# Comparison numbers in PSUM, attention heads in pairs, queries scaled at their eviction: a three-block fp32 kernel on one Trainium2 core

## The chip, the cores and the metric

The kernel runs on one core of one Trainium2 chip. Its time is the device time of one execution in microseconds (us). The core's engines each work through an instruction list of their own and meet only at semaphores: PE (TensorE, matrix products), DVE (VectorE), ACT (ScalarE), POOL (GpSimd) and SP (SyncE, which here issues DMAs). Two on-chip memories matter: SBUF, and PSUM with its eight banks, into which PE writes and from which DVE and ACT read.

## The reference

A first block of two layers, then a second block of one layer. 256 tokens x and 256 context tokens ctx, width 1024, everything in fp32.

```python
# first block, each layer: ffn, mixer, ffn on x (and on ctx in layer 0); the mixer's attention part:
s_loc = einsum(q, k_block) * scale + bias           # scale = 64 ** -0.5 = 0.125, 8 heads of 64
s_ctx = einsum(q, k_ctx) * scale
p = softmax(concat([s_loc, s_ctx]), axis=-1)        # o = p_loc @ v + p_ctx @ v_ctx
# in layer 0 the context too attends to itself:
p = softmax(einsum(q, k) * scale); o = p @ v
# second block: retention, a sparse attention, then the expert retrieval:
s = einsum('btphd,phnd->btphn', q, subkeys)         # 8 heads, 2 halves, 128 keys
v, i = top_k(s, 16)
cand = v[..., 0, :, None] + v[..., 1, None, :]      # 256 pairs a head
cidx = i[..., 0, :, None] * 128 + i[..., 1, None, :]
tv, tj = top_k(cand, 16)
eidx = take_along_axis(cidx, tj); w = softmax(tv)   # 8 * 16 = 128 experts a token
a = gelu(einsum(h, w_down[eidx]));  out = einsum(w * a, w_up[eidx])
```

## The kernel before, in words

**Weights.** All weights stream in as units of 128x1024 (512 KB) by DMA. For fp32 accuracy each is split: ACT rounds it to a high part (L174), DVE (L181) or, in one stretch, POOL (L231) subtracts for the low part, and a product is three matmuls (L262, L263, L264). Such a unit is a *down*, *up* or *query* unit below; one of 24 matmuls is worked on in two halves of 12.

**Order.** Nothing schedules at run time. Each class has a method for each engine, whose text is the instruction order; semaphores hold the engines together. Where side work lies between weight units is set by constants in the text.

**Mixer attention** (`Mix`, L1200 on, once a layer). `MixIn.scalar` (L1182) evicts the projections, queries included, from PSUM. The scores are worked as *items*: one head and 128 queries each; 16 local items (256 local and 256 context keys: 512 columns) in each layer and, in layer 0 alone, 16 context items (256 columns). For an item w: PE makes the scores in bank w % 2 (L1276: a head has 64 channels, so the matmul uses 64 of the array's 128 rows); DVE multiplies by 0.125, adds the bias on the local half (L1376), multiplies the other half (L1377; L1380 for a context item), and takes the maximum (L1383); ACT takes the exponential (L1328, and its sum is read out); DVE normalises (L1391, L1392); PE transposes 128x128 pieces (L1286) into bank 2 or 3; ACT copies them out (L1338); PE multiplies them by the values (L1298, 64 output channels of a head, for two items at once, into bank 4 or 5); ACT moves the result (L1346). The items' order is head by head. Semaphore waits let PE be at most three score items ahead.

**Retrieval** (`Retrieve`, L1955 on). PE runs 16 query units, then K0 = 47 of the 128 down units. Beside the down units the other engines find the experts. DVE takes the top 16 of each head's keys, makes the 256 candidate sums of each head (`pairs`, L2205 and L2208), takes their top 16 (`choose`), and turns the positions into key numbers by comparing with a row of numbers 0 to 127, the iota (`decode`, L2223 to L2238: L2227 is the comparison, L2232 a product, L2234 a sum). `weights` (L2244 to L2246) ends the softmax. All of it is done for two halves of 128 tokens, tt = 0 and 1. Then PE turns the slots (`turn`, L2030), and a dense table of 128 x 128 weights a token is built in 64 *batches* of 4 tokens: DVE *compares* the iota with both key numbers of a slot (L2170, 128x1024 to SBUF), POOL *weighs* one of the two one-hot matrices (L2137, 128x512), PE *spreads* (L2039: 4 matmuls, their outer products, in one of banks 4 to 7) and ACT *keeps* the result (L2082). Compare may run six batches ahead of the spread, by the buffers.

**Constants.** From down unit ALONE = 22 on there is one batch per half unit, for 16 units; then PAUSE = 2 units without any; then two batches per half until K0, which is 7 units; the last 4 batches follow alone. In this whole stretch POOL both weighs and subtracts (L231), until the last units, whose subtraction DVE does. `turn(0)` stands at the end of unit ALONE-1. The second half's `choose` and `decode` run on DVE between comparisons of the first half's batches (`more`). After that `Experts` works through the other 81 down units and 128 up units. Down results of `Retrieve` go to DRAM and come back later (47 of each).

Of the kernel before, what the change touches and what calls it, by code (L numbers as in the profile page):

```python
# [21 lines left out]
ALU = mybir.AluOpType  # L22
# [3 lines left out]
P = 128  # L26
# [372 lines left out]
A_POOL = A_PT + 2048  # L399
# [717 lines left out]
class MixIn:  # L1117
# [60 lines left out]
    def scalar(self, act):  # L1178
# [23 lines left out]
class Mix:  # L1202
    def __init__(self, chip, layer, last, mix_in):
# [3 lines left out]
        self.sc, self.pt = chip.part(A_SC, 4, 512), chip.part(A_PT, 2, 4, S)  # L1207
# [7 lines left out]
        self.items = [(g, h, qt) for g in range(ng) for h in range(NA_H) for qt in range(2)]  # L1215
        n = len(self.items)
        self.scored, self.scores_read, self.maxed, self.exped, self.probs, self.turned, self.copied = (
            s.take(n) for s in (chip.scored, chip.scores_read, chip.maxed, chip.exped, chip.probs, chip.turned, chip.copied))
        self.product, self.moved, self.mixed = chip.product.take(n // 2 + 1), chip.moved.take(n // 2), chip.mixed.take(1)
        self.y_there = chip.y_there.take(2)  # L1220

    def keys(self, g):
        return (0, T2) if g == 0 else (S, T2)

# [40 lines left out]
    def tensor(self, pe):  # L1265
# [4 lines left out]
        def scores(w):  # L1270
            g, h, qt = items[w]
            lo, hi = keys(g)
            po, q0 = 64 * (h % 2), g * S + qt * P
            if w >= 2:
                pe.wait_ge(self.scores_read.sem, self.scores_read.at(w - 1))
            nc.tensor.matmul(chip.bank[w % 2][:, 0:hi - lo], u[po:po + 64, CH_Q + h // 2, q0:q0 + P],  # L1276
                             u[po:po + 64, CH_K + h // 2, lo:hi], start=True, stop=True)\
                .then_inc(self.scored.sem, 1)
# [11 lines left out]
        def values(n):  # L1290
            g, h, _ = items[2 * n]
            po = 64 * (h % 2)
            pe.wait_ge(self.copied.sem, self.copied.at(2 * n + 2))
            if n >= 2:
                pe.wait_ge(self.moved.sem, self.moved.at(n - 1))
            nkt = (keys(g)[1] - keys(g)[0]) // P
            for kt in range(nkt):
                mm = nc.tensor.matmul(chip.bank[4 + n % 2][po:po + 64, 0:S],  # L1298
# [1343 lines left out]
```

## Time and profile before

| | |
|---|---|
| median of 3 runs | 3045.37 us (3043.37 to 3047.05) |
| profiled execution | 3047.02 us, its span 3045.2 us |
| mean granted PE clock | 0.975 of full speed |
| busy share of the span | PE 94%, DVE 71%, ACT 40%, POOL 18% |
| mixer of layer 0, first score to last values | 562.9 to 642.6 us |
| mixer of layer 1, the same | 1549.4 to 1601.5 us |
| retrieval, first spread to the first matmul of `Experts` | 2221.4 to 2415.4 us |

All times of places are from the start of the span. An engine's busy time is the sum over its instructions; where an instruction waited, the timeline gives the idle time before it and, behind an arrow, the engine and line that released it. A tile name (extension_mixer, arena, bank) covers many buffers: arena is the reused part of SBUF, bank is PSUM. A matmul in fp32 as L1276's and L1298's stands as two records in the timeline, and records that follow each other without a gap may be drawn together, with a count.

### The profile page before, as it was taken

The numbers are of one execution on the slowest core, as the hardware profiler recorded it, in microseconds if no ns is written. First come the engines' busy times: TensorE is split into PE (matmuls) and PEld (weight loads), VectorE is DVE, ScalarE is ACT, GpSimd is POOL, SyncE is SP. The second block draws the span as 40 slices with busy tenths as digits, with TensorE's granted clock in tenths as the row PEclk, the third lists the DMA queues.
The fourth block names the chain that finished last, engine by engine and source line by source line (L and its number), as shares of the span: only waits on it lengthen the run. The fifth ranks groups of instructions, "written<-read, shape, count | busy, mean of one in ns | idle before, by whom it ended". The sixth has DMA issues, their size and how long they took to land. (4 is left out here: it accounts for less than half of the span.)

```text
span 3045.2 us, 40386 instructions
## 1 busy us (share of the span) xinstructions
PE 2862.2 (94%) x15682; PEld 2391.7 (79%) x15682; DVE 2171.0 (71%) x3813; ACT 1225.8 (40%) x2228; POOL 534.0 (18%) x403
## 2 busy tenths in 40 slices
PE   7999999999999999999899999389977899999997
PEld 4888878568888778888859999259967788888886
DVE  2999994558998975657656665446997777777776
ACT  2322243453222342223445455245544444444444
POOL 1111115000111110001400000003899600000000
PEclk9999999999999999999999999689999999999999
DMA  6445542123545454444414555304633356555553
GB/s 237 179 174 193 187 151 90 49 92 137 180 176 197 152 191 163 156 147 160 144 42 140 185 188 168 114 1 140 189 107 100 97 189 192 193 190 189 195 190 118
DMA packets 121295, 463.05 MB, mean 152 GB/s; under 512 B 13456, under 2 KB 26128, under 8 KB 107792
## 3 DMA queue, kind: packets, MB, share of 16 engines
q1 hardware_dynamic: 107280, 359.79, 35.9%
q0 software_dynamic: 13824, 100.67, 8.5%
q8 instruction: 125, 2.05, 0.3%
q14 instruction: 66, 0.54, 0.1%
HBM read 453.20 MB, written 7.21 MB: 151 GB/s over the span
## 5 line engine op out<-in xcount | busy, mean ns | idle before, releaser
L174 ACT ACTIVATE weight_hi<-weight_ring 128x512 fp32r<-128x512 f32 x1272 | 798.6, 631 | 1197.5 <-PE bank L264 1196.0
L181 DVE TENSOR_TENSOR weight_lo<-weight_ring,weight_hi 128x512 fp32r<-128x512 f32 x1154 | 868.7, 756 | 466.8 <-ACT weight_hi L174 465.1
L262 PE MATMUL bank<-operand_hi,weight_hi 128*128 128x256 f32 (+1 forms) x3168 | 1046.7, 330 | 28.5 <-DVE operand_lo L601 13.0
L263 PE MATMUL bank<-operand_lo,weight_hi 128*128 128x256 f32 (+1 forms) x3168 | 1036.8, 327 | 0.0
L264 PE MATMUL bank<-operand_hi,weight_lo 128*128 128x256 f32 (+1 forms) x3168 | 1036.1, 327 | 0.0
L262 PEld LDWEIGHTS bank<-operand_hi,weight_hi 128*128 128x128 f32 x3168 | 606.2, 191 | 95.7 <-issue 21.4
L263 PEld LDWEIGHTS bank<-operand_lo,weight_hi 128*128 128x128 f32 x3168 | 606.3, 191 | 52.7
L264 PEld LDWEIGHTS bank<-operand_hi,weight_lo 128*128 128x128 f32 x3168 | 606.0, 191 | 50.4
L859 DVE SCALAR_TENSOR_TENSOR extension_ffn<-extension_ffn,silu_c 128x512 f32<-128x512 f32 x532 | 388.0, 776 | 1.7
L262 PE MATMUL bank<-hidden_hi_ffn,weight_hi 128*128 128x512 f32 (+1 forms) x704 | 256.6, 364 | 4.0 <-DVE arena L1104 4.0
L263 PE MATMUL bank<-hidden_lo_ffn,weight_hi 128*128 128x512 f32 (+1 forms) x704 | 255.3, 363 | 0.0
L264 PE MATMUL bank<-hidden_hi_ffn,weight_lo 128*128 128x512 f32 (+1 forms) x704 | 255.3, 363 | 0.0
L262 PE MATMUL bank<-weight_hi,act_hi_experts 128*128 128x512 f32 x512 | 214.3, 419 | 0.0
L263 PE MATMUL bank<-weight_lo,act_hi_experts 128*128 128x512 f32 x512 | 200.7, 392 | 0.0
L264 PE MATMUL bank<-weight_hi,act_lo_experts 128*128 128x512 f32 x512 | 200.1, 391 | 0.0
L231 POOL TENSOR_TENSOR weight_lo<-weight_ring,weight_hi 128x512 fp32r<-128x512 f32 x118 | 188.9, 1613 | 50.5 <-ACT weight_hi L174 49.4
L810 POOL DMA_DIRECT2D extension_ffn<-in_w_mods x88 | 53.6, 612 | 715.9 <-DVE extension_ffn L859 589.6
L826 POOL TENSOR_TENSOR mod_lo_ffn<-extension_ffn,mod_hi_ffn 128x1024 fp32r<-128x1024 f32 (+1 forms) x44 | 98.3, 2233 | 428.0 <-ACT mod_hi_ffn L868 428.0
L262 PEld LDWEIGHTS bank<-hidden_hi_ffn,weight_hi 128*128 128x128 f32 x704 | 132.8, 189 | 28.5 <-DVE arena L1104 6.7
L264 PEld LDWEIGHTS bank<-hidden_hi_ffn,weight_lo 128*128 128x128 f32 x704 | 132.8, 189 | 20.8
L263 PEld LDWEIGHTS bank<-hidden_lo_ffn,weight_hi 128*128 128x128 f32 x704 | 132.9, 189 | 20.5
L2170 DVE TENSOR_TENSOR arena<-iota,arena 128x1024 f32<-128x1024 f32 x64 | 121.9, 1927 | 17.2 <-PE bank L2039 16.5
(259 smaller groups left out, 2807.6 us busy)
## 6 DMA issues: line engine op xcount, KB each, us to landing
weight_ring<-in_ffn SPq DMA_DIRECT2D x272, 512.0 KB, 3.5
weight_ring<-in_experts SPq DMA_DIRECT2D x256, 512.0 KB, 3.5
extension_ffn<-in_w_mods POOLq DMA_DIRECT2D x96, 1024.0 KB, 7.6
weight_ring<-in_w_mix SPq DMA_DIRECT2D x56, 512.0 KB, 3.4
weight_ring<-in_w_second SPq DMA_DIRECT2D x52, 512.0 KB, 4.0
spill<-early_retrieve SPq DMA_DIRECT2D x47, 128.0 KB, 3.8
arena<-spill SPq DMA_DIRECT2D x47, 128.0 KB, 3.5
extension_mixer<-in_rel_bias SPq DMA_DIRECT2D x2, 1536.0 KB, 6.7
```

Source lines behind the costliest of these rows:

```text
L174: nc.scalar.activation(self.hi[:, g % 2, h], self.ring[:, g % NS, h], ACT.Copy).then_inc(self.rounded, 1)
L181: self.nc.vector.tensor_tensor(self.lo[:, g % 2, h], self.ring[:, g % NS, h], self.hi[:, g % 2, h].bitcast(F32), ALU.subtract).then_inc(se ...
L231: self.nc.gpsimd.tensor_tensor(self.lo[:, g % 2, h], self.ring[:, g % NS, h], self.hi[:, g % 2, h].bitcast(F32), ALU.subtract).then_inc(se ...
L262: nc.tensor.matmul(out, a_hi, b_hi, start=start and n == 0, stop=False)
L263: nc.tensor.matmul(out, a_hi, b_lo, start=False, stop=False)
L264: last = nc.tensor.matmul(out, a_lo, b_hi, start=False, stop=stop and n == len(pairs) - 1)
L810: pool.dma_start(self.w[:, j, u, :, :], src).then_inc(self.loaded[j].sem, 16)
L826: nc.gpsimd.tensor_tensor(self.lo[:, 0:n], self.flat(j), self.hi[:, 0:n].bitcast(F32), ALU.subtract)\
L859: ins = nc.vector.scalar_tensor_tensor(acc, w, scale, acc, ALU.mult, ALU.add)
L2170: nc.vector.tensor_tensor(self.hots(b), iota[:, :].unsqueeze(1).unsqueeze(1).to_broadcast([P, BATCH, 2, P]), self.columns[:, 0:2, t:t + BA ...
```

## The change

- **Queries.** They are multiplied by 0.125 as ACT evicts them. DVE's two instructions on a local item's scores become an addition of the bias and a copy. A context item needs none any more: the maximum and the exponential read the scores in their bank. PE's next context scores wait for the exponential now, not for DVE's copy.
- **Paired heads.** Items are ordered by pairs of heads, the two heads of a pair next to each other. Their score matmuls, on array rows 0 to 63 and 64 to 127, are issued back to back into two banks out of 0, 1, 6, 7. The value matmuls of four items (two heads, 256 queries) are issued in four parts, one behind each item's transposes, the two heads alternately on columns 0 to 63 and 64 to 127 of bank 4 or 5. There is one move per four items, on 128 partitions. The transposed probabilities have twice the buffers.
- **Numbers in PSUM.** ACT copies the iota once into bank 7; `compare` and `decode` read it there. The spreads have banks 4 to 6 instead of 4 to 7.
- **Constants and order.** K0 is 45 instead of 47, ALONE 20 instead of 22. `pairs(1)` is split: heads 0 to 3 before `weights(0)`, heads 4 to 7 behind it.

PE in the attention of layer 0, steady state, local items (L1276 becomes L1289 in the changed kernel, the scores; L1286 becomes L1299, transposes; L1298 becomes L1315, values). Two items before:

```order
L1276 MATMUL bank<-extension_mixer 128x512
L1286 MATMUL bank<-ident,extension_mixer 128x128 x4
L1276 MATMUL bank<-extension_mixer 128x512
L1286 MATMUL bank<-ident,extension_mixer 128x128 x4
L1298 MATMUL bank<-extension_mixer 64x256 x4
```

and two items now:

```order
L1289 MATMUL bank<-extension_mixer 128x512 x2
L1299 MATMUL bank<-ident,extension_mixer 128x128 x4
L1315 MATMUL bank<-extension_mixer 64x256 x2
L1299 MATMUL bank<-ident,extension_mixer 128x128 x4
L1315 MATMUL bank<-extension_mixer 64x256 x2
```

The number of matmuls is the same; the two score matmuls stand together, and the four of values stand as two pairs, each behind one item's transposes.

DVE before the first comparison of the retrieval (L2205 and L2208 are `pairs`, L2244 to L2246 `weights(0)`, on which PE's `turn(0)` waits). Before:

```order
L2238 TENSOR_TENSOR arena<-arena 128x128
L2205 CAST arena<-arena 128x256
L2208 TENSOR_TENSOR arena<-arena 128x256 x8
L2244 TENSOR_REDUCE arena<-arena 128x8
L2245 RECIPROCAL arena<-arena 128x8
L2246 TENSOR_TENSOR arena<-arena 128x128
L2189 MAX arena<-arena 128x8 x2
L2170 TENSOR_TENSOR arena<-iota,arena 128x1024
```

and now:

```order
L2266 TENSOR_TENSOR arena<-arena 128x128
L2233 CAST arena<-arena 128x256
L2236 TENSOR_TENSOR arena<-arena 128x256 x4
L2272 TENSOR_REDUCE arena<-arena 128x8
L2273 RECIPROCAL arena<-arena 128x8
L2274 TENSOR_TENSOR arena<-arena 128x128
L2236 TENSOR_TENSOR arena<-arena 128x256 x4
L2216 MAX arena<-arena 128x8 x2
L2197 TENSOR_TENSOR arena<-bank,arena 128x1024
```

Four of the candidate sums have gone behind `weights(0)`, and the comparison reads bank instead of iota. The diff, cut to its core:

```diff
-A_POOL = A_PT + 2048
+A_POOL = A_PT + 4096
-            nc.scalar.activation(self.u[:, n, 0:self.width[n]], chip.bank[n % 4][:, 0:self.width[n]], ACT.Copy)\
+            nc.scalar.activation(self.u[:, n, 0:self.width[n]], chip.bank[n % 4][:, 0:self.width[n]], ACT.Copy,
+                                 scale=DH ** -0.5 if CH_Q <= n < CH_K else 1.0)\
                 .then_inc(self.evicted.sem, 1)
...
-        self.items = [(g, h, qt) for g in range(ng) for h in range(NA_H) for qt in range(2)]
+        self.items = [(g, 2 * hp + j, qt) for g in range(ng) for hp in range(NA_H // 2) for qt in range(2) for j in range(2)]
+    def score_bank(self, w):
+        return (0, 1, 6, 7)[w % 4]
...
+        def scores(n):
+            if n >= 2 and 2 * n - 3 < self.local:
+                pe.wait_ge(self.scores_read.sem, self.scores_read.at(2 * n - 2))
+            elif n >= 2:
+                pe.wait_ge(self.exped.sem, self.exped.at(2 * n - 2))
+            for w in (2 * n, 2 * n + 1):
+                g, h, qt = items[w]
+                lo, hi = keys(g)
+                po, q0 = 64 * (h % 2), g * S + qt * P
+                nc.tensor.matmul(chip.bank[self.score_bank(w)][:, 0:hi - lo], u[po:po + 64, CH_Q + h // 2, q0:q0 + P],
+                                 u[po:po + 64, CH_K + h // 2, lo:hi], start=True, stop=True)\
+                    .then_inc(self.scored.sem, 1)
...
+        def values(n, part):
...
+            if part == 0:
+                pe.wait_ge(self.copied.sem, self.copied.at(4 * n + 4))
+                if n >= 2:
+                    pe.wait_ge(self.moved.sem, self.moved.at(n - 1))
+            for j in range(2):
+                h = items[4 * n + j][1]
+                mm = nc.tensor.matmul(chip.bank[4 + n % 2][64 * j:64 * j + 64, 0:S],
+                                      v[:, part + 4 - nkt, h * DH:(h + 1) * DH], self.turned_probs(n, j, part),
+                                      start=(part == 0), stop=(part == nkt - 1))
...
-                nc.vector.scalar_tensor_tensor(s[:, 0:S], bank[:, 0:S], 0.125, bias[:, h, r0:r0 + S], ALU.mult, ALU.add)
-                nc.vector.tensor_scalar(s[:, S:T2], bank[:, S:T2], 0.125, None, ALU.mult)\
-                    .then_inc(self.scores_read.sem, 1)
-            else:
-                nc.vector.tensor_scalar(s[:, 0:n], bank[:, 0:n], 0.125, None, ALU.mult)\
-                    .then_inc(self.scores_read.sem, 1)
-            dve.wait_ge(self.scores_read.sem, self.scores_read.at(w + 1))
-            nc.vector.tensor_reduce(chip.nmax[:, w % 4:w % 4 + 1], s[:, 0:n], AX.X, ALU.max, negate=True)\
+                nc.vector.tensor_tensor(s[:, 0:S], bank[:, 0:S], bias[:, h, r0:r0 + S], ALU.add)
+                nc.vector.tensor_copy(s[:, S:T2], bank[:, S:T2]).then_inc(self.scores_read.sem, 1)
+                dve.wait_ge(self.scores_read.sem, self.scores_read.at(w + 1))
+            nc.vector.tensor_reduce(chip.nmax[:, w % 4:w % 4 + 1], s if g == 0 else bank[:, 0:n], AX.X, ALU.max, negate=True)\
                 .then_inc(self.maxed.sem, 1)
...
-NQ, K0 = 16, 47
-ALONE, PAUSE = 22, 2
+NQ, K0 = 16, 45
+ALONE, PAUSE = 20, 2
...
+        self.iota = chip.bank[7][:, 0:P]
...
-            if b >= 4:
-                pe.wait_ge(self.kept.sem, self.kept.at(b - 3))
+            if b >= 3:
+                pe.wait_ge(self.kept.sem, self.kept.at(b - 2))
...
+            if n == 6:
+                act.wait_ge(self.table.sem, self.table.at(17))
+                nc.scalar.activation(self.iota, chip.iota[:, :], ACT.Copy).then_inc(self.table.sem, 1)
...
-            nc.vector.tensor_tensor(self.hots(b), iota[:, :].unsqueeze(1).unsqueeze(1).to_broadcast([P, BATCH, 2, P]),
+            nc.vector.tensor_tensor(self.hots(b), iota.unsqueeze(1).unsqueeze(1).to_broadcast([P, BATCH, 2, P]),
...
-        pairs(1)
+        pairs(1, 0, PH // 2)
         weights(0)
+        pairs(1, PH // 2, PH)
         choose(1, 0)
```

## Rows read from the trace of the kernel before

**Rows 1.** Windows: stretch, length, busy time (instructions) by engine, clock, DMA.
```profile
560.00:645.00 85.00, 77.08 (x273) 36.26 (x272) 52.14 (x146) 46.73 (x120) 0.00 (x0) 0.92 0.04 13
2220.00:2343.00 123.00, 92.41 (x696) 87.94 (x694) 106.95 (x114) 50.25 (x91) 121.51 (x70) 0.94 0.32 94
...
2414.00:3020.00 606.00, 605.27 (x3475) 522.83 (x3474) 435.98 (x798) 284.52 (x496) 0.00 (x0) 1.00 0.58 187
```

**Rows 2.** PE timeline, local attention: start, us, engine, line, op, [idle, releaser].
```profile
585.71 1.12 PE L1276 MATMUL bank<-extension_mixer 64*128 64x512 f32 x2
...
589.00 0.66 PE L1286 MATMUL bank<-ident,extension_mixer 128*128 128x128 f32 x4 [0.52 <-DVE extension_mixer L1392]
589.58 1.94 PE L1298 MATMUL bank<-extension_mixer 128*64 128x256 f32 x8
```

**Rows 3.** Timeline of DVE, the same stretch.
```profile
586.87 0.43 DVE L1376 SCALAR_TENSOR_TENSOR extension_mixer<-bank,extension_mixer 128x256 f32<-128x256 f32 x1 [1.70 <-PE bank L1276]
...
588.86 0.42 DVE L1376 SCALAR_TENSOR_TENSOR extension_mixer<-bank,extension_mixer 128x256 f32<-128x256 f32 x1
```

**Rows 4.** Timeline of PE, context attention, layer 0.
```profile
619.88 0.44 PE L1286 MATMUL bank<-ident,extension_mixer 128*128 128x128 f32 x2 [0.44 <-DVE extension_mixer L1392]
...
623.38 0.44 PE L1286 MATMUL bank<-ident,extension_mixer 128*128 128x128 f32 x2 [0.43 <-DVE extension_mixer L1392]
```

**Rows 5.** One line's instructions: count, ns min/median/max, first and last start, forms.
```profile
L1376 DVE SCALAR_TENSOR_TENSOR extension_mixer<-bank,extension_mixer x32: 413/418/426, 564.2 to 1592.4; 128x256 f32<-128x256 f32 x32
...
L1328 ACT ACTIVATE extension_mixer<-extension_mixer,nmax x48: 499/721/724, 566.9 to 1593.9; 128x512 f32<-128x512 f32 x32, 128x256 f32<-128x256 f32 x16
L1328 ACT ACTIVATION_READ_ACCUMULATOR extension_mixer<-extension_mixer,nmax x48: 185/187/193, 567.5 to 1594.5; 128x1 f32 x48
...
L1338 ACT ACTIVATE extension_mixer<-bank x48: 383/597/598, 570.3 to 1598.9; 128x512 f32<-128x512 f32 x32, 128x256 f32<-128x256 f32 x16
...
L1777 PE MATMUL bank<-arena x32: 370/370/390, 1999.4 to 2002.7; 64*128 64x15 f32 x32
```

**Rows 6.** The same view, for lines of the retrieval.
```profile
L2170 DVE TENSOR_TENSOR arena<-iota,arena x64: 1211/2054/2311, 2219.0 to 2409.3; 128x1024 f32<-128x1024 f32 x64
...
L2137 POOL TENSOR_TENSOR arena<-arena x64: 1028/2015/2032, 2220.3 to 2411.4; 128x512 f32<-128x512 f32 x64
...
L231 POOL TENSOR_TENSOR weight_lo<-weight_ring,weight_hi x118: 1262/1297/3325, 2096.4 to 2375.1; 128x512 fp32r<-128x512 f32 x118
...
L2208 DVE TENSOR_TENSOR arena<-arena x16: 411/1507/1520, 2156.8 to 2216.6; 128x256 f32<-128x256 f32 x16
```

**Rows 7.** Timeline of PE, expert retrieval, first spread to end.
```profile
2217.91 0.55 PE L2030 MATMUL bank<-ident,arena 128*128 128x128 f32 x3 [4.01 <-DVE arena L2246]
...
2221.42 2.08 PE L2039 MATMUL bank<-arena 128*128 128x128 f32 x8 [0.54 <-POOL arena L2137]
...
2314.64 1.06 PE L2039 MATMUL bank<-arena 128*128 128x128 f32 x8
...
2316.97 1.06 PE L2039 MATMUL bank<-arena 128*128 128x128 f32 x8
...
2333.75 0.36 PE L262 MATMUL bank<-operand_hi,weight_hi 128*128 128x256 f32 x1
...
2343.05 2.13 PE L2039 MATMUL bank<-arena 128*128 128x128 f32 x16 [1.82 <-POOL arena L2137]
...
2382.84 2.15 PE L2039 MATMUL bank<-arena 128*128 128x128 f32 x16
...
2386.26 2.15 PE L2039 MATMUL bank<-arena 128*128 128x128 f32 x16
...
2415.38 0.55 PE L262 MATMUL bank<-operand_hi,weight_hi 128*128 128x256 f32 x1 [0.73 <-issue]
```

**Rows 8.** Timeline of DVE: second half's decoding, its start and end.
```profile
2258.78 1.31 DVE L2223 TENSOR_SCALAR arena<-arena 128x128 uint32<-128x128 uint32 x1
...
2298.49 4.29 DVE L2170 TENSOR_TENSOR arena<-iota,arena 128x1024 f32<-128x1024 f32 x2
```

More of the change, by code:

```diff
@@ L1288, in transposes @@
             mm.then_inc(self.turned.sem, 1)
[L1290 to L1295, printed above, removed]
-            nkt = (keys(g)[1] - keys(g)[0]) // P
-            for kt in range(nkt):
-                mm = nc.tensor.matmul(chip.bank[4 + n % 2][po:po + 64, 0:S],
-                                      v[:, kt + 4 - nkt, h * DH:(h + 1) * DH], pt[:, n % 2, kt, :],
-                                      start=(kt == 0), stop=(kt == nkt - 1))
-            mm.then_inc(self.product.sem, 1)
+        def values(n, part):
+            g, _, _ = items[4 * n]
+            nkt = (keys(g)[1] - keys(g)[0]) // P
+            if part >= nkt:
+                return
+            if part == 0:
[7 more added lines that the diff above has]
+                                      start=(part == 0), stop=(part == nkt - 1))
+            if part == nkt - 1:
+                mm.then_inc(self.product.sem, 1)
         pe.wait_ge(evicted.sem, evicted.at(16))
-        for w in range(3):
-            scores(w)
+        scores(0)
         pe.wait_ge(evicted.sem, evicted.at(20))
+        scores(1)
         for w in range(len(items)):
-            if w + 3 < len(items):
-                scores(w + 3)
+            ahead = w // 2 + 2
+            early = 2 * ahead - 3 < self.local
+            if w % 2 == 0 and ahead < len(items) // 2 and early:
+                scores(ahead)
             transposes(w)
-            if w >= 2 and w % 2 == 0:
-                values(w // 2 - 1)
-        values(len(items) // 2 - 1)
+            if w % 2 == 0 and ahead < len(items) // 2 and not early:
+                scores(ahead)
+            if w >= 4:
+                values(w // 4 - 1, w % 4)
+        for part in range(4):
+            values(len(items) // 4 - 1, part)
         pe.wait_ge(self.mixed.sem, self.mixed.at(1))
@@ L1354, in scalar @@
             copies(w)
-            if w >= 3 and w % 2 == 1:
-                move(w // 2 - 1)
-        move(len(items) // 2 - 1)
-        act.wait_ge(self.product.sem, self.product.at(len(items) // 2 + 1))
+            if w >= 8 and w % 4 == 1:
+                move(w // 4 - 2)
+        move(len(items) // 4 - 2)
+        move(len(items) // 4 - 1)
+        act.wait_ge(self.product.sem, self.product.at(len(items) // 4 + 1))
         for b in range(2):
@@ L2082, in keep @@
             nc.scalar.activation(self.weight[:, BATCH * b:BATCH * (b + 1), :].rearrange("p a b -> p (a b)"),
-                                 chip.bank[4 + b % 4][:, :], ACT.Copy).then_inc(self.kept.sem, 1)
+                                 chip.bank[4 + b % 3][:, :], ACT.Copy).then_inc(self.kept.sem, 1)
         def exp(tt):
@@ L2201, in best, with pairs @@
                 dve.wait_ge(chip.dve_step.sem, chip.dve_step.base)
-        def pairs(tt):
-            step(nc.vector.tensor_copy(ixf[:, tt, :, :], ix[:, tt, :, :]))
+        def pairs(tt, first, last_h):
+            if first == 0:
+                step(nc.vector.tensor_copy(ixf[:, tt, :, :], ix[:, tt, :, :]))
             vp = v[:, tt, :, :].rearrange("p (h two) k -> p h two k", two=2)
-            for h in range(PH):
+            for h in range(first, last_h):
                 last = nc.vector.tensor_tensor(
```

52 lines of the change are left out of this document (25 added, 27 removed).

## The prediction

> **What bounds the kernel now.** I read the windows first [rows 1]. In the Experts stage PE is busy for 605.27 of 606 us: what stands there costs its full time. In the mixer of layer 0 it is busy 77.08 of 85 us, at a granted clock of 0.92, with DVE at 52.14: neither is full. From 2220 to 2343, in the retrieval, PE is busy 92.41 of 123 us and POOL 121.51: there POOL sets the pace. Then the timelines. In the mixer's local part PE waits 0.52 us for DVE's normalisation before a transpose [rows 2] and DVE waits 1.70 us for scores once in two items [rows 3]: each waits for the other in turn. Two items take 5.68 us: 2 x 1.99 (the distance from one item's first DVE instruction to the next) + 1.70 [rows 3]. In the context part two items take 3.50 us [rows 4]. In the retrieval the durations of one instruction stand far apart [rows 6]: the comparison L2170 takes 1.21 us at least and 2.05 in the median, the weighing L2137 1.03 or 2.02, the subtraction L231 1.26 to 3.33. A DVE instruction with two inputs in SBUF and a POOL instruction lengthen each other. When DVE rested (2311 to 2320), a half unit with its spread took 2.33 us, 2314.64 to 2316.97 [rows 7].
>
> **The mixers.** Bias addition and copy replace two DVE instructions of the same shape, L1376 at 0.42 us being the row for both sorts: I take their saving as nothing. What can change is the 1.70 us. PE's work for two items is two score matmuls (1.12 each, drawn as two records), two sets of transposes (0.66 each) and the values (1.94) [rows 2]: 5.5 as drawn, 5.2 without its 0.52 of waiting, since drawn times overlap a little (5.68 - 0.52). If both kinds of pairs ran side by side it would be 1.12 + 1.32 + 0.97 = 3.4, and with scores alone 4.4; DVE needs 3.98. So with both side by side DVE is the bound and the 1.70 goes; with scores alone most of it does. For side by side speaks L1777, on alternating halves of the rows: 32 matmuls of 0.37 us each within 3.6 us [rows 5], a third of their sum; but pipelined matmuls are drawn overlapped anyhow, and its halves of columns no row shows. Local items: 5.68 - 3.98 = 1.70 a pair, 8 pairs a layer: 13.6 at best. In layer 1 I take 12; in layer 0 only 9, since a clock of 0.92 [rows 1] and the first items' filling hold PE back there. Context items: four take 7.0 us now [rows 4]. ACT will be their bound, an exponential of 0.50 with 0.19 of reading its sum and a copy of 0.38 [rows 5], with a quarter of a move of about the copy's length 1.16 an item, 4.6 for four. 4 x (7.0 - 4.6) = 9.6, and 1 at the passage from local to context, whose items now go without a DVE copy: 10.5. The exponential may cost more or less from a bank; the copy L1338 reads one already and costs less than the exponential, so I take no difference. Sum of the mixers: -31.5. Bounds: -36 with both layers at the full 13.6 plus 9.6, and -11 if nothing runs side by side and only the reordering (0.5 a pair over 16 pairs) and part of the context's copy count.
>
> The Trainium skill, "TensorEngine Tiling (Array Packing)", Key Properties, says that tiles work in parallel, but that changing the tiling mode drains TensorE. Here the mode changes around each pair. By the first half of the rule the sum stands; by the second each change costs something that no row here isolates, and the time moves to the first rival's.
>
> **The comparison from PSUM.** 64 comparisons of 128x1024. The price of one from a bank is in no row. From below, 1.21 (the shortest from SBUF, no POOL beside it); from above 2.05, if nothing is freed. DVE reads a bank and SBUF in L1376, 256 elements in 0.413 us at least [rows 5]; L2208, two SBUF inputs of the same shape, takes 0.411 at least [rows 6]. So a bank costs nothing more by itself, and I take 1.22. The Trainium skill, "Perfetto Trace Analysis", Optimizing Scalar/DVE Operations, gives DVE some 125 ns of access overhead on PSUM against 60 on SBUF; by it the comparison would be 1.28 and 64 of them 4 us more, though hidden where PE sets the pace; the rows show 0.002 of difference, and I go by them.
>
> Does it free POOL? L2208 takes 0.41 at least and 1.51 in the median [rows 6], two SBUF inputs beside POOL's work; the same holds for L2170. L1376-like instructions stand beside no POOL work, so that a bank operand is free of it is inferred, not seen. The Trainium skill, "GPSIMD Engine Reference", Specifications, says that GpSimd's SBUF interface is shared with VectorE, with contention when a DVE instruction has two SBUF inputs or runs in a two-port mode. The comparison would then be out of it; the trace agrees as far as it goes (1.21 against 2.05).
>
> **The retrieval, step by step.** *Start* (places here are in the span of before, the mixers' gain apart). turn(0) waited 4.01 us for weights(0) [rows 7]; with two units less before it PE will wait there for 6 us more, or less by what DVE gains. DVE gains 0.8 us or more on each of the two decoding comparisons L2227. Four of the eight L2208 go behind weights(0), so that turn(0) comes sooner, but still ahead of the first comparison: they only fill the time of the turn and its eviction, about 0.5. And where PE waits, POOL runs out of subtractions, and the L2208 fall from 1.51 towards 0.41 [rows 6]: up to 4 us more. I put spread(0) at 2216.7 instead of 2221.42 [rows 7], between 2215.5 and 2218.7. *The 32 single batches.* Now 2221.42 to 2333.75, 112.3 us [rows 7]. PE's 2.33 a half is the floor, POOL's uncontended 1.04 + 1.27 = 2.31 just under it: 32 x 2.33 = 74.6. The decoding of the second half holds DVE from 2258.78 to 2298.49, 39.7 us, with 8 comparisons in it [rows 8]. With 8 x 0.83 less (2.05 to 1.22) and as much for each of two L2227, which have twice the elements (a cautious count), it is 31.4, or 3.9 a half, slower than PE by 12.8 over 8 halves; six batches of lead can hide that in part. 74.6 at best, 87.4 at worst; I take 82, nearer to the worst, since choose(1) keeps DVE from building much lead. *Pause*: 5 half units of 12 matmuls between spreads, 2333.75 to 2343.05, of which 1.82 was waiting for POOL [rows 7] and goes: 7.5, or 1.5 a half unit. *14 halves with two batches.* The stretch shows 3.42 a half once POOL has no subtraction left, 2382.84 to 2386.26 [rows 7]. POOL will need 2 x 1.04 + 1.27 = 3.35, DVE 2.5: 14 x 3.42 = 47.9. *The last 4*, from the last half to the first matmul of Experts: DVE alternates comparison 1.22 and subtraction 0.68, 1.9 each; 7.6 in all. So Experts begin at 2216.7 + 82 + 7.5 + 47.9 + 7.6 = 2361.7 instead of 2415.38 [rows 7]: -53.7. Three spread banks instead of four ask only that a batch be kept within three, and ACT needs 0.6 of each 2.33: nothing. The copy of the iota, one ACT instruction under query units: nothing. *Given back.* Two down units less stand before Experts and two more in it, where PE is full: 4 half units of 1.5 = 6.0. Retrieval: -47.7, bounds -57 (lead hides all, spread(0) early) and +2 (nothing is freed).
>
> **Sum.** 3047.02 - 31.5 - 47.7 = 2967.8 for the profiled execution, which stands 1.65 above the median of the runs shown; so 2966 as a median.
>
> **The rivals.** *A, the pairs don't run side by side.* For it: no row shows halves of columns in parallel, nor scores of 512 columns; PE then needs about 5.2 for two items and stays the bound. Mixers -11: 2986 to 2987. *B, POOL isn't freed* or the comparison is as long beside it. Against it is the sharp split of 1.04 and 2.02. The retrieval keeps its pace; the earlier start (-4) and the 6.0 given back leave +2: 3047 - 31.5 + 2 - 1.65 = 3016. *C, slower: the comparison from a bank is long.* Its broadcast read, the same numbers again for each slot, is no contiguous read as L1376's. The whole table then hangs on DVE: from spread(0) to Experts 64 x t plus some 62 us (the 194 of now, less 64 x 1.93, a mean between the median and the shorter ones [rows 6], is 70, of which 8 is waiting that falls away), against 194 now. Minus 31.5 and 5 of the start and plus 6, break-even is at t = (194 + 30.6 - 62) / 64 = 2.54; at 3.2, half as long again as the median now, the time is 3047 + 73 + 6 - 31.5 - 5 = 3089. Against it: 0.413 in [rows 5] and nothing near 2.5. *A and B together*: 3036.
>
> **Chances.** Forecast 0.60 (own range 2950 to 2980), A 0.18, B 0.12, A and B 0.04, C 0.03, and 0.03 for faster than 2950. The range of 8 in 10 is 2948 to 3002: it takes in A and the slower part of the forecast's costs and leaves out B's side. A difference under 0.2% (6 us) can't be told from none; faster 0.95, same 0.02, slower 0.03.
>
> **What would show it.** Local items 4.0 us apart per two, with DVE's 1.70 gone (A: 5 us, score records one behind another); context items at about 2.3 per two with ACT nearly full. The comparison (L2197 of the changed kernel) at 1.2 us in the median, the weighing always 1.04 (B: both still near 2); no waits of PE for POOL from unit ALONE on; Experts starting 85 us earlier in the span than before (31.5 + 53.7), and taking 6.0 us longer. The prediction is wrong if PE waits for more than 12 us at turn(0), if DVE's decoding holds back all 32 halves, or if the granted clock in these stretches falls to the lower level for long because PE now waits differently.

## The result, and the profile after

| | before | changed |
|---|---|---|
| median of runs | 3044.51 us (3043.37 to 3047.05, 4 runs) | 2948.94 us (2947.35 to 2950.94, 4 runs) |
| ratio | | 0.9685, 95% interval 0.9673 to 0.9697 |
| profiled execution | 3047.02 us | 2947.35 us |
| busy in the span: PE, DVE, ACT, POOL | 2862.2, 2171.0, 1225.8, 534.0 us | 2798.8, 2109.9, 1219.2, 464.5 us |

96 us faster; 2966 was forecast, 79 less than before. 2948.94 lies below the forecast's own range (2950 to 2980), in the part that it gave 0.03 to, and inside the range of 8 in 10 (2948 to 3002) by 1 us. The two profiled executions lie 99.7 us apart, one at the slow end of its runs, the other at the fast end. Where those 99.7 went, by the distance between equal places of the two spans, against the forecast's terms:

| stretch | forecast | traces |
|---|---|---|
| mixer of layer 0 | -19.5 | -25.1 |
| mixer of layer 1 | -12.0 | -14.5 |
| between it and the query units | 0 | -0.3 |
| start: to the first spread | -4.7 | -8.5 |
| 32 single batches and the pause | -32.1 | -32.9 |
| double batches and the last 4 | -16.8 | -22.1 |
| Experts | +6.0 | +3.7 |
| sum | -79.2 | -99.7 |

**Windows of the changed kernel**, columns as in [rows 1]: the mixer of layer 0, the single batches, Experts.

```profile
560.00:645.00 85.00, 72.44 (x367) 41.81 (x366) 58.18 (x153) 54.25 (x133) 2.24 (x4) 0.96 0.21 81
2173.00:2256.00 83.00, 78.19 (x648) 77.29 (x649) 76.42 (x106) 46.23 (x84) 76.33 (x64) 0.98 0.42 128
2312.00:2918.00 606.00, 606.00 (x3510) 524.85 (x3511) 437.34 (x799) 286.99 (x501) 0.00 (x0) 1.00 0.58 188
```

In the retrieval POOL is down from 121.51 of 123 us to 76.33 of 83 and PE up to 78.19 of 83: PE sets the pace. Experts is full of PE's work, as it was.

**PE in the local items**, the timeline that answers to [rows 2]:

```profile
584.34 1.13 PE L1289 MATMUL bank<-extension_mixer 64*128 64x512 f32 x4
585.40 0.66 PE L1299 MATMUL bank<-ident,extension_mixer 128*128 128x128 f32 x4
585.98 0.65 PE L1315 MATMUL bank<-extension_mixer 128*64 128x256 f32 x4
587.12 0.66 PE L1299 MATMUL bank<-ident,extension_mixer 128*128 128x128 f32 x4 [0.48 <-DVE extension_mixer L1415]
```

Two matmuls of scores, four records, take 1.13 us, where one, two records, took 1.12. Four records of values take 0.65 where eight took 1.94. PE waits 0.48 us for DVE's product, once in two items. DVE [rows 3] no longer waits for scores: from one item to the next it takes 1.98 us, without a gap.

```profile
585.00 0.42 DVE L1403 TENSOR_TENSOR extension_mixer<-bank,extension_mixer 128x256 f32<-128x256 f32 x1
...
586.98 0.42 DVE L1403 TENSOR_TENSOR extension_mixer<-bank,extension_mixer 128x256 f32<-128x256 f32 x1
```

**Context items** [rows 4]: two items that have value matmuls beside them take 2.53 us (602.06 to 604.59, 609.17 to 611.70), two without take 2.04 (607.13 to 609.17), in which PE waits 0.60 for DVE's product. Before, two took 3.50.

```profile
602.06 0.70 PE L1289 MATMUL bank<-extension_mixer 64*128 64x256 f32 x4
...
604.59 0.70 PE L1289 MATMUL bank<-extension_mixer 64*128 64x256 f32 x4
...
607.13 0.70 PE L1289 MATMUL bank<-extension_mixer 64*128 64x256 f32 x4
...
608.80 0.44 PE L1299 MATMUL bank<-ident,extension_mixer 128*128 128x128 f32 x2 [0.60 <-DVE extension_mixer L1415]
609.17 0.70 PE L1289 MATMUL bank<-extension_mixer 64*128 64x256 f32 x4
...
611.70 0.70 PE L1289 MATMUL bank<-extension_mixer 64*128 64x256 f32 x4
```

The value matmuls run four items late, so the first four context items still carry those of the last local ones. In that stretch PE has no gap:

```profile
596.00:608.00 12.00, 12.00 (x80) 5.53 (x76) 7.42 (x28) 9.11 (x33) 0.00 (x0) 1.00 0.00 0
```

**The comparison and the weighing** of the changed kernel, the view of [rows 6]: the two medians are 1.21 and 1.04, where they were 2.05 and 2.02.

```profile
L2197 DVE TENSOR_TENSOR arena<-bank,arena x64: 1198/1212/1226, 2170.6 to 2307.6; 128x1024 f32<-128x1024 f32 x64
...
L2164 POOL TENSOR_TENSOR arena<-arena x64: 1028/1041/3016, 2171.9 to 2308.9; 128x512 f32<-128x512 f32 x64
```

**The retrieval on PE**, answering to [rows 7]: turn(0), the first spread, two spreads where the second half's decoding begins, the first matmul of the pause, doubles, the last batches, the first matmul of Experts.

```profile
2168.60 0.90 PE L2054 MATMUL bank<-ident,arena 128*128 128x128 f32 x3 [4.56 <-DVE arena L2274]
...
2172.97 1.16 PE L2063 MATMUL bank<-arena 128*128 128x128 f32 x8 [0.91 <-POOL arena L2164]
...
2201.37 1.06 PE L2063 MATMUL bank<-arena 128*128 128x128 f32 x8
...
2203.70 1.06 PE L2063 MATMUL bank<-arena 128*128 128x128 f32 x8
...
2253.90 0.36 PE L262 MATMUL bank<-operand_hi,weight_hi 128*128 128x256 f32 x1
...
2261.70 2.13 PE L2063 MATMUL bank<-arena 128*128 128x128 f32 x16 [0.37 <-POOL arena L2164]
...
2265.10 1.95 PE L2063 MATMUL bank<-arena 128*128 128x128 f32 x16
...
2268.32 1.96 PE L2063 MATMUL bank<-arena 128*128 128x128 f32 x16
...
2303.77 3.74 PE L2063 MATMUL bank<-arena 128*128 128x128 f32 x32
2308.69 1.13 PE L2063 MATMUL bank<-arena 128*128 128x128 f32 x8 [1.19 <-POOL arena L2164]
...
2311.91 0.35 PE L262 MATMUL bank<-operand_hi,weight_hi 128*128 128x256 f32 x1 [0.73 <-issue]
```

The steps are 2.33 us (2201.37 to 2203.70) in the single batches and 3.22 (2265.10 to 2268.32) in the double ones. Experts begin at 2311.91 instead of 2415.38.

### The profile page after: what moved, and what is told of

It reads as the page before. It is cut to its first block and busy times, and to the rows that moved or that the text cites. A ratio compares the mean times of both kernels' runs of the same rounds, so it can differ in the third digit from the quotient of the medians.

```text
span 2945.5 us, 40330 instructions
## 1 busy us (share of the span) xinstructions
PE 2798.8 (95%) x15682; PEld 2359.6 (80%) x15682; DVE 2109.9 (72%) x3801; ACT 1219.2 (41%) x2217; POOL 464.5 (16%) x399
## 3 DMA queue, kind: packets, MB, share of 16 engines
q8 instruction: 125, 2.05, 0.3%
## 5 line engine op out<-in xcount | busy, mean ns | idle before, releaser
L231 POOL TENSOR_TENSOR weight_lo<-weight_ring,weight_hi 128x512 fp32r<-128x512 f32 x114 | 150.6, 1330 | 54.1 <-ACT weight_hi L174 52.7
L263 PEld LDWEIGHTS bank<-hidden_lo_ffn,weight_hi 128*128 128x128 f32 x704 | 132.9, 189 | 20.5
L262 PEld LDWEIGHTS bank<-weight_hi,act_hi_experts 128*128 128x128 f32 x512 | 95.9, 187 | 37.7 <-DVE act_lo_experts L272 12.0
```

The source lines that it names most:

```text
L231: self.nc.gpsimd.tensor_tensor(self.lo[:, g % 2, h], self.ring[:, g % NS, h], self.hi[:, g % 2, h].bitcast(F32), ALU.subtract).then_inc(se ...
L262: nc.tensor.matmul(out, a_hi, b_hi, start=start and n == 0, stop=False)
L263: nc.tensor.matmul(out, a_hi, b_lo, start=False, stop=False)
```

## The experiments

The runs of one group ran on one chip beside the kernel before; what a kernel is worth against the changed one is taken from the ratios to the kernel before.

### The parts alone

**The iota back in SBUF** (three spread banks, constants and order as changed):

```diff
-        iota16, iota = self.iota[:, 0:TOPK], self.iota
+        iota16, iota = chip.iota[:, 0:TOPK], chip.iota[:, :]
```

> The changed kernel with one thing undone: comparison and decoding read the iota in SBUF again (three spread banks, constants and order stay). Theory (the bank operand frees POOL and DVE of each other): the retrieval goes back to its old pace, comparison near 2.05 us and weighing near 2.0 in the median; the mixers keep their 40 us; about 3044.5 - 40 + 2 = 3006 us, between 3000 and 3012. Rival (the order, the split of pairs and the constants brought the retrieval's gain): 2950 to 2962 us.

Measured: 3005.37 us (ratio 0.9863, 0.9847 to 0.988). The page for the two lines, in the same view as above, shows the medians of before again:

```profile
L2197 DVE TENSOR_TENSOR arena<-iota,arena x64: 1206/2055/2314, 2176.2 to 2366.4; 128x1024 f32<-128x1024 f32 x64
...
L2164 POOL TENSOR_TENSOR arena<-arena x64: 1032/2016/2028, 2177.5 to 2368.6; 128x512 f32<-128x512 f32 x64
```

So this one operand carries 1.8% (0.9863 against 0.9685), some 54 us: that DVE and POOL hold each other up less is most of the retrieval's gain (59.8 in the table, from the start to Experts).

**The iota in a bank, and nothing else,** in the kernel before: ACT's copy, `self.iota` at the three places, banks `4 + b % 3`, `kept.at(b - 2)`; K0 = 47, ALONE = 22, `pairs(1)` whole, the mixers as before.

> The kernel before with the iota in a bank alone (three spread banks; K0 = 47, ALONE = 22, pairs(1) whole, mixers as before). Theory: the single batches 33 us shorter, the double ones and the last four 22, the start 4 to 6, the low clock at the start of Experts 2: about 2983 us, 2979 to 2987. Rival: constants and split carry a part of the gain of more than 10 us: above 2993 us.

Measured: 2984.69 us (ratio 0.9799, 0.9783 to 0.9815), 61.4 below the 3046.11 of before. Its DVE timeline at the start shows the decoding comparison at 2.29 us, but the eight candidate sums at 8.12, as long as before:

```profile
2186.21 2.29 DVE L2231 TENSOR_TENSOR arena<-bank,arena 128x2048 f32<-128x2048 f32 x1
...
2204.73 8.12 DVE L2212 TENSOR_TENSOR arena<-arena 128x256 f32<-128x256 f32 x8
```

**The mixers alone**: the file of the changed kernel up to the line `NQ, K0 = 16, ...`, from there on that of before.

> The mixers of the changed kernel with the retrieval of before. Theory: the spans of the two traces add up, 25.1 us from layer 0 and 14.5 from layer 1: 3044.5 - 40 = 3004.5 us, 3002 to 3007. Rival (the retrieval takes part of it back, as a transfer or the clock falls differently): above 3010 us.

Measured: 3008.16 us (ratio 0.9875, 0.9859 to 0.9892), 38.0 below before. The two parts add up to 99.4 on this chip, and the whole change measured 95.6 and 96.6 in its two comparisons. And the kernel with the iota in SBUF, which differs from this one by K0, ALONE, the split of pairs and the three banks, lies 2.8 below it. Neither of these differences, of opposite sign, is larger than the intervals: the constants and the order brought nothing that can be measured.

### The pairs of heads

**Neither rows nor columns in pairs**: the items' order within a pair of heads is head, query half, and each head's values are issued in turn.

```diff
-        self.items = [... for hp in range(NA_H // 2) for qt in range(2) for j in range(2)]
+        self.items = [... for hp in range(NA_H // 2) for j in range(2) for qt in range(2)]
...
-            for j in range(2):
-                h = items[4 * n + j][1]
+            for m in (2 * part, 2 * part + 1):
+                j, kt = m // nkt, m % nkt
+                h = items[4 * n + 2 * j][1]
...
-            at = S * (w % 2) + P * qt
+            at = S * (h % 2) + P * qt
```

> The changed kernel with items in the order head, query half within a pair of heads, so that back-to-back score matmuls use the same 64 rows, and with each head's value matmuls issued in turn, so that neighbours use the same columns. Banks, buffers, scaling, the move and all counts stay. Theory (the mixers' gain is matmuls running side by side): PE needs about 5.1 us for two local items and sets the pace; local items lose 1.1 us a pair over 16 pairs and context items about 1 a pair over 8: 26 us, about 2975 us, between 2968 and 2982. Rival (the deeper banks and the absent DVE copies brought it): at most 8 us lost, under 2957 us.

Measured: 2974.97 us (ratio 0.9766, 0.975 to 0.9783), 25 above the changed kernel. So of the mixers' 39.6 us, 25 are the pairs'; the other 15 go with what this run keeps (two banks of scores more, values in four parts, queries scaled at their eviction, no DVE copy for context items), and no run parts these from each other. The PE timeline of its local items: the same records, but the two scores take 1.98 us and a part of values 1.08, one behind another; two items are 5.1 apart (586.50 to 591.60).

```profile
586.50 1.98 PE L1289 MATMUL bank<-extension_mixer 64*128 64x512 f32 x4
...
589.00 1.08 PE L1316 MATMUL bank<-extension_mixer 128*64 128x256 f32 x4
...
591.60 1.12 PE L1289 MATMUL bank<-extension_mixer 64*128 64x512 f32 x2
```

**Only the values in turn** (the middle part of that diff, with `items[4 * n + j]`; scores stay paired):

> The changed kernel with the value matmuls of one head in turn instead of alternating between the halves of columns (same places, same counts, same buffers); the scores stay paired on halves of rows. By the traces a part of four records takes 0.65 us alternating and 1.08 in turn: PE needs 0.43 more a part, 0.86 for two local items, and then about 4.2 us against DVE's 3.96. Theory: columns run side by side as rows do, and of the 26 us that both together are worth 6 to 10 are the columns': 2955 to 2959 us. Rival (halves of columns don't run side by side; rows alone did it): within 2 us of 2949.

Measured: 2956.43 us (ratio 0.9704, 0.969 to 0.9719), about 6 above the changed kernel. The number fell where it was expected, but the place is another. By the starts of DVE's maxima the sixteen local items of layer 0 take 30.0 us (29.8 in the changed kernel) and those of layer 1 28.7 (28.4): PE needs 4.25 us for two (586.27 to 590.52), DVE 3.96, and PE's lead hides the difference over eight pairs. The context items take 23.6 us instead of 18.4: where PE has no gap, two items take 3.38 us instead of 2.53, the full 2 x 0.43.

```profile
606.16 0.70 PE L1289 MATMUL bank<-extension_mixer 64*128 64x256 f32 x4
...
609.54 0.70 PE L1289 MATMUL bank<-extension_mixer 64*128 64x256 f32 x4
```

**Only the scores on the same rows** (the first and last part of the diff; values stay on alternating columns):

> The changed kernel with items in the order head, query half, so that neighbouring score matmuls use the same 64 rows; the values stay alternating on halves of columns. Two local items' scores take 1.98 us instead of 1.13: again 0.85 more for PE, all before the transposes. Theory: 2955 to 2962 us, and with the values' run the two don't add up to 26, since DVE hides the first part of either. Rival (only columns matter): within 2 us of 2949.

Measured: 2966.31 us (ratio 0.974, 0.9725 to 0.9755), about 16 above, more than expected. In the local items PE's work is the same as with the values in turn, 4.25 us for two. Its score rows:

```profile
586.17 1.98 PE L1289 MATMUL bank<-extension_mixer 64*128 64x512 f32 x4
...
590.42 1.98 PE L1289 MATMUL bank<-extension_mixer 64*128 64x512 f32 x4
```

What differs is the clock. Windows of the start of the attention in layer 0 (the third number from the right is the granted clock), first the values in turn, then the same rows:

```profile
564.00:580.00 16.00, 11.02 (x46) 4.59 (x44) 14.56 (x37) 12.26 (x26) 0.00 (x0) 0.89 0.11 34
```

```profile
564.00:580.00 16.00, 13.20 (x34) 6.16 (x34) 13.13 (x33) 11.01 (x23) 0.00 (x0) 0.76 0.10 34
580.00:596.00 16.00, 16.00 (x62) 6.82 (x61) 12.50 (x33) 8.07 (x21) 0.00 (x0) 0.82 0.00 1
```

(With the values in turn it is 1.00 in the second window; with neither paired 0.73 and 0.84.) With the values in turn the clock is at its lower level (1.2 GHz) for (1 - 0.89) x 16 / 0.5 = 3.5 us, with the same rows for 7.7 + 5.8 = 13.5, and in layer 1 for none against 13.7 (0.62 over 18 us): 24 us more at half speed, worth up to 12 us of PE's work. The local items of the two layers take 35.4 and 34.2 us against 30.0 and 28.7, 10.9 more: PE has no lead left after the slow stretch. The context items take 20.5, 3.1 less. The medians lie 10 apart, the two profiled executions 6.1.

### The constants and the order of the start

The changed kernel itself ran once more as the measure of this group:

> The changed kernel itself, on the same chip as the three beside it, as their measure: ratio to the kernel before 0.9685 within 0.001.

Measured: 2948.97 us (ratio 0.9682, 0.9668 to 0.9695).

```diff
-NQ, K0 = 16, 45
-ALONE, PAUSE = 20, 2
+NQ, K0 = 16, 47
+ALONE, PAUSE = 22, 2
```

> The changed kernel with K0 = 47 and ALONE = 22 again, all else kept. PE waits 4.56 us at turn(0) and 0.91 at the first spread in the changed kernel. Theory 1: two down units more before turn(0) fill that wait, and Experts, where PE is full, lose two: 4 to 5 us faster than the changed kernel. Theory 2: with PE busy there, the ring keeps moving and POOL goes on subtracting beside DVE's chain to weights(0), which lengthens by up to 4 us as before: within 1.5 us of the changed kernel.

Measured: 2947.10 us (ratio 0.9675, 0.9662 to 0.9689). PE's waits at turn(0) and at the first spread, in its timeline:

```profile
2173.82 0.55 PE L2054 MATMUL bank<-ident,arena 128*128 128x128 f32 x3 [2.01 <-DVE arena L2274]
...
2178.19 1.05 PE L2063 MATMUL bank<-arena 128*128 128x128 f32 x7 [2.40 <-POOL arena L2164]
```

They sum to 4.4 us, against 5.5 in the changed kernel (4.56 and 0.91, above); two units of 2.9 were to fill them. The DVE timeline shows what kept them open: four candidate sums ahead of weights(0) take 5.69 us, 2.49 in the changed kernel.

```profile
2166.80 5.69 DVE L2236 TENSOR_TENSOR arena<-arena 128x256 f32<-128x256 f32 x4
```

POOL goes on subtracting beside them: in the changed kernel POOL has one subtraction left from 2165 on; here nine follow each other from 2159.40 to 2173.62. The second theory holds in mechanism; whether 1.9 us are won can't be told within these intervals.

**One unit** (K0 = 46, ALONE = 21):

> K0 = 46 and ALONE = 21, all else as in the changed kernel. Theory 1: one unit of 2.9 us more in the wait of 4.56: 2.9 us faster than the changed kernel. Theory 2 (POOL's further subtractions lengthen DVE's chain): within 1 us.

Measured: 2947.03 us (ratio 0.9676, 0.9663 to 0.9689). Neither theory can be told from the other by it.

**pairs(1) whole**, before `weights(0)`:

> The changed kernel with pairs(1) whole before weights(0). The second four candidate sums take 1.42 us in the changed kernel's trace and are followed by 0.75 of maxima; turned round they delay turn(0) by 1.4 us, and the turn and its eviction then stand alone before the first comparison. Theory: 1 to 2 us slower than the changed kernel. Rival (the first comparison comes after all eight either way, so that only the eviction's 0.5 shows): within 0.7 us.

Measured: 2947.74 us (ratio 0.9677, 0.9663 to 0.969). That is 1.2 below the changed kernel and within the intervals: no 1 to 2 us of loss is seen, and the split is worth nothing that could be measured.

**The decoding alone from SBUF**:

```diff
-        iota16, iota = self.iota[:, 0:TOPK], self.iota
+        iota16, iota = chip.iota[:, 0:TOPK], self.iota
```

> The changed kernel with the decoding's comparison alone reading SBUF (L2255), the 64 batches' comparison still the bank. L2255 takes 3.2 us again instead of 2.29, twice before turn(0) and twice in the second half's decoding. Theory: 2 to 4 us of PE waiting more, 2951 to 2953 us; nearly all of the 56 us is the 64 comparisons'. Rival (the decoding is what held the single batches back): above 2960 us.

Measured: 2952.64 us (ratio 0.9695, 0.968 to 0.971), about 3 above the changed kernel and inside the intervals. The 64 comparisons of the batches carry nearly all of the 54.

### A version that beats both

K0 = 46, ALONE = 21, and on DVE in the mixers the reciprocal between copy and maximum:

```diff
+        def invert(w):
+            dve.wait_ge(self.exped.sem, self.exped.at(w + 1))
+            r = chip.rsum[:, w % 4:w % 4 + 1]
+            chip.dve_step.passed(1)
+            nc.vector.reciprocal(r, r).then_inc(chip.dve_step.sem, 1)
...
                 nc.vector.tensor_copy(s[:, S:T2], bank[:, S:T2]).then_inc(self.scores_read.sem, 1)
+            if beside is not None:
+                invert(beside)
...
-            in_order(dve, chip.dve_step, nc.vector.reciprocal(r, r))
+            dve.wait_ge(chip.dve_step.sem, chip.dve_step.base)
```

> A version meant to beat the changed kernel: K0 = 46 and ALONE = 21, and in the mixers the reciprocal of item w stands between the copy and the maximum of item w + 2, so that neither of DVE's two waits for its own result stands open (0.12 between copy and maximum, 0.04 between reciprocal and product, in 1.98 an item). Theory (DVE is the bound of the local items): 0.15 x 32 items = 4.8 us less in the mixers and 1.9 from the constants as measured: about 2943 us. Rival (the chain from scores over exponential to transposes is the bound, and a later maximum lengthens it): not under 2947.

Measured: 2939.85 us (ratio 0.9649, 0.9636 to 0.9662), 9 to 11 us below the changed kernel by times and ratios, more than forecast. One item on DVE:

```profile
584.37 0.42 DVE L1409 TENSOR_TENSOR extension_mixer<-bank,extension_mixer 128x256 f32<-128x256 f32 x1
...
585.04 0.15 DVE L1398 RECIPROCAL rsum<-rsum 128x1 f32<-128x1 f32 x1
585.15 0.69 DVE L1415 TENSOR_REDUCE nmax<-extension_mixer 128x1 f32<-128x512 f32 x1
...
586.15 0.42 DVE L1409 TENSOR_TENSOR extension_mixer<-bank,extension_mixer 128x256 f32<-128x256 f32 x1
```

An item takes 1.78 us (584.37 to 586.15), 0.20 less: both waits for its own results are covered. That is 0.20 x 32 = 6.4 us at most. The trace shows 4.6 in the two mixers (562.90 to 617.17 and 1524.28 to 1561.47 in the changed kernel, 563.71 to 615.29 and 1523.76 to 1559.07 here): one item in each layer takes 2.28 and 2.64, and the context items gain 0.3. With the constants' 1.9 this makes 6.5; where the rest of the 9 to 11 comes from isn't shown, and the profiled execution (2944.45) was the slowest of the five.

## Why the prediction was right, and by how much not

**How near it was.** The mechanism was right in both parts, and the sizes were too small in both. The mixers gave 39.6 us, beyond the bound of 36; the retrieval with the two units given back 59.8, beyond the bound of 57. The signs to look for were off in the same way: Experts start 103.5 us earlier, not 85, and PE still waits for POOL (0.91, 2.87, 1.72, 0.37 and 1.19 us), where no wait was forecast. That the time lies inside the range of 8 in 10, by 1 us, is luck.

**Bound of the mixers.** Right for the local items: pairs run side by side, on rows and on columns, PE falls under DVE, DVE's 1.70 us goes, and an item takes 1.98. Rival A was priced at -11 for the mixers; with no pairs they gave about 15, and the 25 us of that run are what A would have taken. For the context items ACT was to be the bound, with 4.6 us for four. Four take 4.57 once the local values are done (607.13 to 611.70), so the number fits, but ACT isn't the bound: it is busy for 9.11 of 12 us from 596 to 608 and PE for all 12, and every item with values became longer by the full 0.43 when the values went in turn. Where no values stand beside them PE waits 0.60 for DVE's product, and none of the three engines is full. PE's work in the context items was never added up in the prediction. The whole context part went from 27.8 to 18.4 us, 9.4 less, where 10.5 was forecast. ACT's exponential from the bank takes 0.47, from SBUF 0.50.

**The clock in the mixers: the term that was mis-sized.** The forecast took 1.6 and 4.6 us off the steady state's 13.6 for a lower clock and the filling, as if that stayed. It didn't. Windows of the start of the attention, before and changed:

```profile
564.00:580.00 16.00, 14.89 (x31) 5.74 (x30) 10.83 (x27) 9.05 (x20) 0.00 (x0) 0.58 0.11 33
```

```profile
564.00:580.00 16.00, 10.29 (x48) 4.81 (x48) 15.39 (x40) 11.90 (x27) 0.00 (x0) 0.89 0.09 34
```

(1 - 0.58) x 16 / 0.5 = 13.4 us at the lower level before, 3.5 now; in layer 1, by like windows, 10.2 (0.68 over 16) and 3.4 (0.86 over 12). That is 10 and 7 us less at half speed, while PE had been nearly fully busy in them (14.89 of 16): up to 5 and 3.5 us, and the traces show 5.6 and 2.5 more than forecast: in layer 0 the local items gave 15.0 us (44.8 to 29.8) where 9 were forecast, and the context items took 1.1 of that back. More rest didn't mean a lower clock here: from 564 to 572 PE is busy for 6.9 of 8 us before and 3.5 of 8 in the changed kernel. In layer 0 the lower level lasts 10.2 us in the run with the iota alone, whose mixers are those of before, and 13.5 to 13.8 in the two runs with the scores on the same rows; in the ten with paired rows it lasts 3.5 us or, in three of them, doesn't come. The run with the same rows differs from the changed kernel only in the items' order, so the pairing of rows shortens the stretch; in what way stays open.

**The start.** Forecast -4.7, bounds -2.7 to -5.9, measured -8.5, outside them. The step that was too small is the sum on DVE ahead of the first comparison. Its timeline before, all eight candidate sums in one row:

```profile
2208.87 8.10 DVE L2208 TENSOR_TENSOR arena<-arena 128x256 f32<-128x256 f32 x8
```

and in the changed kernel (first decoding comparison, the sums, the first comparison of a batch):

```profile
2145.70 2.29 DVE L2255 TENSOR_TENSOR arena<-bank,arena 128x2048 f32<-128x2048 f32 x1
...
2165.16 2.49 DVE L2236 TENSOR_TENSOR arena<-arena 128x256 f32<-128x256 f32 x4
...
2168.46 1.42 DVE L2236 TENSOR_TENSOR arena<-arena 128x256 f32<-128x256 f32 x4
...
2170.59 1.20 DVE L2197 TENSOR_TENSOR arena<-bank,arena 128x1024 f32<-128x1024 f32 x1
```

The sums take 2.49 + 1.42 = 3.9 us instead of 8.10, the whole way from decoding comparison to batch comparison 24.9 instead of 33.4 (2185.63 to 2219.02). Only "up to 4 us" of it was priced; of the 4.7 forecast, some 2.6 are left for it beside the decoding's 1.6 and the 0.5 of the order. But the run with K0 = 47 shows that this isn't a gain of its own: the sums are short because PE stands still, units stop being used and POOL runs out of subtractions. The 5.5 us that PE waits (4.6 before) are the other side of it. The advance before spread(0) and two units less of work are one trade.

**The single batches.** Forecast 82 us for 32, from the first spread to the pause; measured 80.9 (2172.97 to 2253.90). The floor of 2.33 was taken from one undisturbed half unit and holds for almost all; the decoding took DVE 30.2 us (2202.70 to 2232.93, the start of the comparison behind it) where 31.4 was reckoned. PE waits for POOL three times in this stretch, 0.91, 2.87 and 1.72 us. The longest stands behind L2260, the decoding's product, which still has two SBUF inputs:

```profile
2202.70 4.42 DVE L2251 TENSOR_SCALAR arena<-arena 128x128 uint32<-128x128 uint32 x1
...
2213.00 2.28 DVE L2260 TENSOR_TENSOR arena<-arena 128x2048 f32<-128x2048 f32 x1
```

The weighing that begins 0.16 us after it on POOL:

```profile
2213.16 3.02 POOL L2164 TENSOR_TENSOR arena<-arena 128x512 f32<-128x512 f32 x1 [1.19 <-DVE arena L2197]
```

It takes 3.02 us and ends 0.9 after the product (2215.28); its shortest is 1.03, so nearly all of its work falls behind the product's end, and the spread that waited 2.87 follows at 2216.32. And L2251, one input of 128x128, takes 4.42 us while POOL works through four instructions back to back, none of them lengthened; its shortest of four is 0.22. So the lengthening isn't confined to two inputs from SBUF, as the prediction had it; a small instruction with a single one was held longer.

**Double batches and the last four.** Forecast 55.5 us, measured 50.2. The 3.42 of a half had been read as PE's own; the changed kernel takes 3.22. In the row 2382.84 of [rows 7] its 16 matmuls stand drawn as one piece of 2.15 us; in the changed kernel they take 1.96. Between the two batches 0.2 of waiting was hidden in what looked like a floor. The 13 steps from 2261.70 to 2303.77 take 42.1 instead of 44.5. The rest is the end: the last four batches with their half unit take 8.1 (2303.77 to 2311.91), where 3.4 + 7.6 was reckoned: two of the four follow the half unit's own batches without a wait (32 matmuls in one piece), since the comparisons were ahead.

**Experts.** Two more down units cost 3.7 and not 6.0: before, Experts began at the lower clock (0.71 in the window 2414 to 2424, [rows 7] shows its first matmul at 0.55 us), and now at the full one (0.35, above).

**The rivals.** B, POOL not freed, was priced at +2 for the retrieval without the relief; the run with the iota in SBUF gave 3005 against the 3016 of the forecast, 11 less, most of it from the mixers being 8 us better than forecast. C, a long comparison: the broadcast read of a bank costs 1.21 us, the same as from SBUF undisturbed. The rule on DVE's access overhead for PSUM (the Trainium skill, "Perfetto Trace Analysis", Optimizing Scalar/DVE Operations) would have had 1.28, by the prediction's estimate. The shortest is 1.198 from the bank, above, and 1.211 from SBUF [rows 6], so the measurement decides against a difference here. The rule on the shared interface (the Trainium skill, "GPSIMD Engine Reference", Specifications) is borne out by the first experiment for two SBUF inputs. L2251 has one, and would fall under the rule's other case, a two-port mode; no trace names the mode that an instruction ran in, so that half isn't shown.

## What to carry to other kernels

Where VectorE and GpSimd work side by side, look at the spread between the shortest and the median duration of one instruction: here 1.21 against 2.05 us and 1.03 against 2.02 meant that they held each other up, and moving a single constant operand into PSUM gave both back their time. Matmuls of 64-channel heads took somewhat over half the time (1.13 us against 1.98, 0.65 against 1.08) when two of them were issued back to back on the two halves of rows, or of columns. An expected number that comes true says nothing of where the time went: the values in turn cost the 6 us foreseen, but in the context items and not in the local ones. Before a steady-state time is called a floor, look inside rows that are drawn as one: a wait of 0.2 us between merged matmuls counted in each of 13 steps here.

## What the runs showed of the hardware that was not expected

- One GpSimd instruction beginning beside a VectorE one with two SBUF inputs took 3.02 us instead of 1.04 and ended 0.9 after it; a VectorE instruction of 0.23 us with one SBUF input took 4.42 beside four of GpSimd's in a row.
- At the start of the attention the granted clock stayed at the lower level for 10.2 to 13.8 us in layer 0 with neighbouring score matmuls on the same rows (the kernel before, the iota alone, the same rows, no pairs), and for 3.5 at most with scores paired on both halves (the ten other runs).
- Two matmuls of 64 rows side by side, 64x512 each, took 1.13 us against 1.12 for one; two of 64 columns on the two halves of columns, 128x256 each, took 0.65 against 1.08 for two on the same columns.
- DVE lost 0.20 us an item to two waits for its own results, covered by nothing more than another order.
